# A state-space scan whose small matmuls move between the products of a projection

## The reference

```
proj = h @ w_in[layer]
u, q, k, v, f_logit, g_ssm, g_att = jnp.split(proj, IN_SPLITS, axis=-1)
...
xr = jnp.einsum('blgh,gph->blgp', ug, br)
xi = jnp.einsum('blgh,gph->blgp', ug, bi)
...
_, _, sr, si = lax.associative_scan(_complex_affine_combine, (lr, li, xr, xi), axis=1)
y = (jnp.einsum('blgp,ghp->blgh', sr, c_re.astype(f32))
     - jnp.einsum('blgp,ghp->blgh', si, c_im.astype(f32)))
y = y.reshape(bsz, seq, SSM_WIDTH) + d_skip.astype(f32) * u32
y = jax.nn.gelu(y).astype(u.dtype)
```

## Time and profile before

| | us |
|---|---|
| median of 3 runs | 3455.22 (3454.71 to 3459.01) |
| profiled execution, span | 3463.4 |
| entry and scan, up to the last product of turn 7 | about 208 of it |
| PE busy over the whole span | 3252.7 (94%) |
| PE idle at the start of the scan stage | 6.9 |
| PE waiting for POOL at turn 4 | 3.3 |

### The profile page before, as it was taken

One profiled execution on the slowest core, in us unless ns is written; L12 is line 12 of the kernel. 1 busy time (PEld: TensorE's weight loads), 2 busy tenths in 40 slices (PEclk: granted clock), 3 DMA queues, 4 the chain that ended last, 5 costly groups with the idle time before them and its releaser, 6 DMA issues. The chain is left out here.

```text
span 3463.4 us, 48142 instructions
## 1 busy us (share of the span) xinstructions
PE 3252.7 (94%) x16380; PEld 2680.7 (77%) x16380; DVE 1826.3 (53%) x3756; ACT 1303.2 (38%) x2179; POOL 1334.0 (39%) x830
## 2 busy tenths in 40 slices
PE   7999999898889999999999987899999988999999
PEld 6867787798888888888888854478888864478887
DVE  7404324887748777777777377432212336642211
ACT  4234433245543333333334334333322215633322
POOL 2323352288862222222221323434444316734443
PEclk9889999999999999999999998799999988999999
DMA  5321242244569999999997310023323420023332
GB/s 121 81 70 32 73 109 75 60 153 172 197 240 341 323 325 317 332 317 325 322 321 242 82 49 25 9 83 97 97 85 99 118 55 1 1 86 97 97 90 80
DMA packets 453881, 502.00 MB, mean 145 GB/s; under 512 B 77409, under 2 KB 398241, under 8 KB 435825
## 3 DMA queue, kind: packets, MB, share of 16 engines
q1 hardware_dynamic: 430448, 363.77, 34.3%
q0 software_dynamic: 18432, 134.23, 10.5%
q10 hardware_dynamic: 4864, 2.23, 0.3%
HBM read 458.06 MB, written 38.80 MB: 143 GB/s over the span
## 5 line engine op out<-in xcount | busy, mean ns | idle before, releaser
L125 POOL TENSOR_TENSOR w_low<-w_ring,w_high 128x1024 fp32r<-128x1024 f32 (+3 forms) x317 | 758.2, 2395 | 1136.4 <-ACT w_high L120 1108.8
L136 PE MATMUL ps<-h_low,w_high 128*128 128x512 f32 (+1 forms) x2432 | 918.5, 378 | 54.1 <-POOL w_low L125 28.3
L137 PE MATMUL ps<-h_high,w_high 128*128 128x512 f32 (+1 forms) x2432 | 900.6, 370 | 0.0
L138 PE MATMUL ps<-h_high,w_low 128*128 128x512 f32 (+1 forms) x2432 | 900.5, 370 | 0.0
L136 PEld LDWEIGHTS ps<-h_low,w_high 128*128 128x128 f32 x2432 | 464.0, 191 | 125.9 <-POOL w_low L125 31.8
L137 PEld LDWEIGHTS ps<-h_high,w_high 128*128 128x128 f32 x2432 | 463.9, 191 | 63.8 <-issue 6.3
L138 PEld LDWEIGHTS ps<-h_high,w_low 128*128 128x128 f32 x2432 | 462.9, 190 | 56.9
L120 ACT ACTIVATE w_high<-w_ring 128x1024 fp32r<-128x1024 f32 (+3 forms) x317 | 323.9, 1026 | 123.6 <-PE ps L138 120.0
L136 PE MATMUL ps<-v_low,top 128*128 128x512 f32 x768 | 299.7, 390 | 6.6 <-DVE v_low L125 6.6
L138 PE MATMUL ps<-v_high,top_at 128*128 128x512 f32 x768 | 300.8, 392 | 0.0
L137 PE MATMUL ps<-v_high,top 128*128 128x512 f32 x768 | 300.7, 392 | 0.0
(11 more groups left out here) (538 smaller groups left out, 5452.7 us busy)
## 6 DMA issues: line engine op xcount, KB each, us to landing
w_ring<-in_peer_uv_dram SPq DMA_DIRECT2D x128, 512.0 KB
u_raw<-in_peer_uT_dram SPq DMA_DIRECT2D x78, 512.0 KB, 6.0
w_ring<-in_peer_uT_dram SPq DMA_DIRECT2D x50, 512.0 KB, 3.8
gates<-peer_gates SPq DMA_DIRECT2D x31, 768.0 KB, 11.4
w_ring<-in_ffn_w_gate_dram SPq DMA_DIRECT2D x44, 512.0 KB, 3.7
w_ring<-in_ffn_w_up_dram SPq DMA_DIRECT2D x44, 512.0 KB, 3.7
w_ring<-in_w_in_dram SPq DMA_DIRECT2D x36, 512.0 KB, 3.8
w_ring<-in_ffn_w_down_dram SPq DMA_DIRECT2D x32, 448.0 KB, 3.8
```

Of the source, the lines that this page charges most:

```text
L125: return eng.tensor_tensor(rounded(low), whole, high, ALU.subtract)
L136: nc.tensor.matmul(out, rounded(w_high), rounded(x_low), start=start, stop=False, **more)
L137: nc.tensor.matmul(out, rounded(w_high), rounded(x_high), start=False, stop=False, **more)
L138: return nc.tensor.matmul(out, rounded(w_low), rounded(x_high), start=False, stop=stop, **more)
```

## The change

`product` gets an argument `beside`, a function that is called behind each of its first two matmuls and that the tile loop calls twice more behind the third. Through it the 64 matmuls of the kernel stand in the two tiles of turn 1, four to a k step, and the 96 matmuls of the outputs in both tiles of turn 5 and the first of turn 6. The last k step's third matmul signals the tile before the small ones behind it. ACT moves the kernel after turn 1 (`move_kernel`), issues the band after turn 2 and does the gelus after turn 6. On DVE the product of the skip weights goes first, into another buffer, and the fill and the addition go between the steps up and the steps down. The read of u moves from the end of the entry to the head of SP's stream in the scan (`load_u`), ahead of the weight loads. The wait for `y_saved` moves from the end of the scan to `load_y`. Since pieces of work now stand around most turns, the turns are written out, all but turns 3 and 4.

```
-def product(nc, out, w_high, w_low, x_high, x_low, start, stop, **more):
+def product(nc, out, w_high, w_low, x_high, x_low, start, stop, beside=None, **more):
     nc.tensor.matmul(out, rounded(w_high), rounded(x_low), start=start, stop=False, **more)
+    if beside is not None:
+        beside(0)
     nc.tensor.matmul(out, rounded(w_high), rounded(x_high), start=False, stop=False, **more)
+    if beside is not None:
+        beside(1)
     return nc.tensor.matmul(out, rounded(w_low), rounded(x_high), start=False, stop=stop, **more)
...
-                mm.then_inc(mm_done, 1)
+                                 beside=(lambda at, i=i, b=b, k=k: beside[i, b](pe, 4 * k + at)) if given else None)
+                    if k == w.kt[b] - 1:
+                        mm.then_inc(mm_done, 1)
+                    if given:
+                        beside[i, b](pe, 4 * k + 2)
+                        beside[i, b](pe, 4 * k + 3)
...
-            sp.wait_ge(u_saved, 16 * SSM_T)
-            by_group = u_dram.rearrange("t (g h) (r s) -> r h (t g) s", h=SSM_H, r=PH)
-            for r in range(PH):
-                at = (PH - 1 - r) * SSM_H
-                sp.dma_start(tb.u[at:at + SSM_H, :, :], by_group[r]).then_inc(tb.u_in, 16)
...
+        def kernel_of(tile):
+            def beside(pe, at):
+                n = 32 * tile + at
+                p, x, two = n // 4, n // 2 % 2, n % 2
+                half = HALF[two]
+                mm = nc.tensor.matmul(c.ps[:, 6 + two, p * SSM_H:(p + 1) * SSM_H], tb.reach[half, x, p, :], tb.c[x][half, p, :], start=x == 0, stop=x == 1)
+                if p == PAIRS - 1 and x == 1:
+                    mm.then_inc(kernel_done, 1)
+            return beside
+
+        def load_u(sp):
+            sp.wait_ge(tb.u_saved, 16 * SSM_T)
+            by_group = tb.u_dram.rearrange("t (g h) (r s) -> r h (t g) s", h=SSM_H, r=PH)
+            for r in range(PH):
+                at = (PH - 1 - r) * SSM_H
+                sp.dma_start(tb.u[at:at + SSM_H, :, :], by_group[r]).then_inc(tb.u_in, 16)
...
+        def outputs_of(tile):
+            def beside(pe, at):
+                n = 32 * tile + at
+                p, part = n // 6, n % 6
+                if n == 0:
+                    pe.wait_ge(banded, 16 * PH)
+                    pe.wait_ge(moved, 4)
+                if n == 2:
+                    pe.wait_ge(carried, 2)
+                    pe.wait_ge(swept, total[0])
...
-        project_copy(c, w_qk, qkT, ahead, before={"dve": sweeps}, after={"sp": lambda sp: sp.wait_ge(y_saved, 16 * 4)},
-                     between={1: {"pe": fill, "act": move}, 4: {"act": band}, 6: {"pe": outputs, "act": gelus}})
+        project_copy(c, w_qk, qkT, ahead, before={"sp": load_u, "dve": sweeps},
+                     between={1: {"pe": fill, "act": move}, 2: {"act": move_kernel}, 3: {"act": band}, 5: {}, 6: {}, 7: {"act": gelus}},
+                     beside={(1, 0): kernel_of(0), (1, 1): kernel_of(1), (5, 0): outputs_of(0), (5, 1): outputs_of(1), (6, 0): outputs_of(2)})
...
         def load_y(sp):
+            sp.wait_ge(y_saved, 16 * 4)
```

More of the change, by code:

```diff
@@ L462, with project @@
 Programs = namedtuple("Programs", "sync gpsimd tensor scalar vector slots_free")
-def project(c, w, evacuate, rhs=None, ahead=None, whole=None, before={}, after={}, norm=None, between={}, unrolled=(), alternate=False):
+def project(c, w, evacuate, rhs=None, ahead=None, whole=None, before={}, after={}, norm=None, between={}, unrolled=(), alternate=False, beside=None):
     with c.stage() as ctx:
-        one = projection(c, ctx, w, evacuate, rhs, ahead, whole, before, after, norm, between, unrolled, alternate)
+        one = projection(c, ctx, w, evacuate, rhs, ahead, whole, before, after, norm, between, unrolled, alternate, beside=beside)
         with c.nc.Block() as block:
@@ L769, in tile_of, with project_copy @@
     return buf[:, i * per_turn + b, :]
-def project_copy(c, w, dest, ahead=None, before={}, after={}, norm=None, between={}):
+def project_copy(c, w, dest, ahead=None, before={}, after={}, norm=None, between={}, beside=None):
     nc = c.nc
@@ L780, in act @@
             split(b)
-    project(c, w, {"act": act}, ahead=ahead, before=before, after=after, norm=norm, between=between)
+    project(c, w, {"act": act}, ahead=ahead, before=before, after=after, norm=norm, between=between, beside=beside)
 def project_scaled(c, w, dest, ahead=None, before={}):
@@ L1847, in ssm @@
         entry(c, A, tables, w_u, w_qk, qkT)
-        scan(c, tables, w_qk, ahead, qkT, ygT, y_dram)
+        scan(c, tables, w_qk, ahead, qkT, ygT, y_dram, y_saved)
 class EntryNorm:
@@ L2143, in entry, with scan @@
                 after={"pe": lambda pe: turn(pe, range(KD, GROUPS)), "act": rest_moved, "sp": store_u})
-def scan(c, tb, w_qk, ahead, qkT, ygT, y_dram):
+def scan(c, tb, w_qk, ahead, qkT, ygT, y_dram, y_saved):
     nc = c.nc
@@ L2173, in fill @@
                         mm.then_inc(filled, 1)
-            for p in range(PAIRS):
-                for x in range(2):
-                    for two, half in enumerate(HALF):
-                        mm = nc.tensor.matmul(c.ps[:, 6 + two, p * SSM_H:(p + 1) * SSM_H], tb.reach[half, x, p, :], tb.c[x][half, p, :], start=x == 0, stop=x == 1)
-                        if p == PAIRS - 1 and x == 1:
-                            mm.then_inc(kernel_done, 1)
+        def kernel_of(tile):
[13 more added lines that the diff above has]
+                sp.dma_start(tb.u[at:at + SSM_H, :, :], by_group[r]).then_inc(tb.u_in, 16)
         def move(act):
@@ L2270, in sweeps @@
                 all_step(level, False)
+            dve.wait_ge(kernel_out, 2)
+            v.memset(tb.toeplitz, 0.0).then_inc(cleared, 1)
+            dve.wait_ge(diagonal, 1)
+            v.tensor_tensor(tb.kernel[0:SSM_H, :, :], tb.kernel[0:SSM_H, :, :], mine, ALU.add).then_inc(diagonal, 1)
             for level in range(LEVELS - 2, -1, -1):
```

62 lines of the change are left out of this document (28 added, 34 removed).

## The result

| | before | after |
|---|---|---|
| median of four runs each | 3456.12 us | 3521.55 us (3519.21 to 3523.30) |
| ratio | | 1.0181 (95% interval 1.0166 to 1.0195) |
| profiled execution, span | 3463.4 us | 3517.4 us |
| ACT's first squares of q and k, in the next stage, from the span's start | 217.85 us | 283.58 us |

The account below looks back on a forecast made before the run. PE was taken as the bound, held up by blocks of small matmuls that lower its clock and by waits. Terms -2.6 + 31.6 - 0.6 - 3.7 = +24.7 us gave 3480 us, own range 3470 to 3490, with rivals 3454 to 3508.

Parts of the forecast that it names:

- entry, turn 0 starts: End of the entry: with the reads of u behind the barrier, the next stage starts earlier, -2.6 us, bounds 0 to -2.6.
- turn 1 with its slow tail: Turn 1 with kernel matmuls in slots: the clock falls to 0.50 after 4.6 us; 21.6 becomes 53.2 us, +31.6.
- POOL's wait and its slow stretch: PE's 3.28 us wait for POOL and the slow clock behind it mostly go: -3.7 us, bounds -4.9 to 0.
- outputs with their slow tail: Three output tiles with matmuls in slots: 51.8 becomes 51.2 us, -0.6, if the clock stays up.
- I take the clock as staying up, just more likely than not: Outputs: full clock assumed because small matmuls are longer and a third have the products' shape; at 0.50, +27 us.
- third rival: The clock falls in the outputs too: up to +27 us more, 3508 us, or 3494 if midway; chance 0.28.
- slot's price: Small matmuls between products: 0.46 us for one kernel matmul, 0.51 for two; at clock 0.50, 0.66 and 0.77.
- the loads: Turn 1's weight loads behind u's eight reads (4.8 us of SP): costed at nothing, covered by 22.8 us.
- second rival: Full clock throughout, in turn 1 too: +5.4 us, 3461 us, not told from no change; chance 0.13.
- DVE's slack: Outputs wait for DVE's sweeps: 26 us with the fill against 33 us of turns 2 to 4; slack 7, cost nothing.
- weight load 0.32 us after its product's start: Sign to look for: a 64-row matmul's weight load starts about 0.32 us after its product's start, not with it.
- first rival: Switches hide: loads of the other shape run behind products, 0.056 us an instruction; -27.6 us, 3428 us; chance 0.12.

Follow-up runs that it names:

- the run with the kernel in a block: The changed kernel with the kernel's 64 matmuls back in a block behind the span states, the outputs still beside the products: 3487.29 us, 1.0075 of before.
- u read second: The changed kernel with all four small matmuls behind the third product and SP's reads of u behind turn 1's weight loads: 3441.20 us, 0.9954 of before.
- the run with 128: The changed kernel with the same slots, but kernel and carry matmuls taking all 128 array rows, not 64 (time only): 3447.37 us, 0.9968 of before.

## Why the prediction was wrong, step by step

The sign was right, and so was the mechanism in turn 1: a slot's switch, and the clock that falls with it. The forecast had the clock wrong in the outputs and took a slot as too cheap: +25 forecast, +65 measured, outside the range. By stages, from the two traces (and the earlier trace rows):

| term | predicted | measured |
|---|---|---|
| entry, turn 0 starts (58.59, now 56.48) | -2.6 | -2.1 |
| fill, to the first kernel matmul or turn 1 | 0 | +3.8 |
| turn 1 with its slow tail (21.6, now 56.7 + 1.8) | +31.6 | +36.9 |
| POOL's wait and its slow stretch | -3.7 | -4.9 |
| outputs with their slow tail (51.8, now 80.0 + 2.6) | -0.6 | +30.7 |
| behind them, to the next stage | 0 | +1.3 |
| sum | +24.7 | +65.7 |

**The step that failed** is "I take the clock as staying up, just more likely than not" in the outputs. It fell 13.7 us in and stayed at 0.50 for 66 us. That is the prediction's third rival, chance 0.28, priced at up to +27 more; it measured 31.3 more than the forecast's term. The reason given was that the small matmuls are longer there and a third has the products' shape. It did not hold the clock: in the run with the kernel in a block it went after 5.6 us, as in turn 1 (5.7). For turn 1 I had taken the block's behaviour as nearest; the same reading for the outputs, whose block fell within 3.7 us, would have given 3508, the upper end of the range. What puts the measured time above that end are the two terms that follow, the slot's price (5.3 us in turn 1 and some 4 in the outputs) and the loads (3.8).

**The slot's price** was mis-sized. Slot by slot, product to product less a product alone (0.23 and 0.43):

| slot | predicted, full | measured | predicted, 0.50 | measured |
|---|---|---|---|---|
| one kernel matmul | 0.46 | 0.52 | 0.66 | 0.83 |
| two | 0.51 | 0.53 | 0.77 | 0.84 |
| one carry | 0.49 | 0.56 | 0.71 | 0.91 |
| one on u | 0.28 | 0.25 to 0.36 | 0.33 | 0.42 to 0.45 |

At the full clock the estimate from attention's 2-row matmuls was 0.02 to 0.07 short for the matmuls of 64 rows. At 0.50 it was 0.07 to 0.20 short. For a single kernel matmul the sum had 0.41 us from its load to the next product, taken from a block, and 0.53 were seen (110.98 to 111.51); the rest of the 0.17 lies before the load, where I had kept the 0.09 us. That in a block the neighbours hide part of a small matmul's load is my reading, which no run tests. Fourteen k steps of turn 1 at 3.79 us in place of 3.38 are 5.7 us, the whole miss of that term. With the outputs at 0.50 throughout, three k steps take 11.04 us and not 9.86.

How the loss divides, by an estimate from these distances: at the full clock throughout, the slots as measured would make turn 1 36.2 us (48 x 0.75, +14.6) and the outputs 54.1 (8 x 6.76, +2.3). So of the 67.6 us of both terms 17 are switches and 51 the lower clock; the second rival's 3461 would have been 3470 even so.

**The loads.** "I cost that at nothing" was wrong by 3.8 us: 2.5 of more waiting for `reachT`, and the rest the transposes at the low clock behind it. The cover of 22.8 us was counted for PE's want of the weights; but ACT wants them first, at 64.44, 18 us ahead of PE's turn 1 (82.57), and stands in front of the moves of `reachT`. I named what was queued behind the reads on SP, not what was queued behind the late weights on ACT. Nor is it so that nobody wants u until the fill is over: the span states, inside the fill, read it (1.6 us of PE's wait in u read second).

**POOL** went as said, at the end of its bounds: no PE wait for it, -4.9. **DVE's slack** held: the last step down ends at 168.8 and the outputs start at 173.7, 5 us for the 7 predicted. **Turn 0** is earlier by 2.1 for 2.6. The sign "weight load 0.32 us after its product's start" was seen at 0.43. The first rival, switches that hide behind the products, is refuted: a small load of 64 rows starts 0.43 us after its product's start, where the next product in a row would have started at 0.23. The Trainium skill ("TensorE: Matmul & The Clock Gate", Step-by-step) says that PE pulls weight loads ahead of matmuls in flight when the row groups don't conflict or the load targets the background weight buffer. The traces agree where the rows are equal, 0.08 us after the product's start in the run with 128; between products of 128 rows and matmuls of 64 no load is seen ahead, and no run shows which of the two conditions is missing. The Trainium skill ("TensorEngine Tiling (Array Packing)", Key Properties) also says that a change of the tiling mode drains TensorE. The traces agree with that: a single slot costs 0.52 us with the change and 0.22 without.

## What to carry to other kernels

Small matmuls put between large ones cost mostly by changes of shape, there and back: at the full clock 0.5 us for one or two of 64 rows here, 0.25 us for each further two, and 0.22 us for one that has the products' rows. So if they have to stand among products, let them stand in longer rows, but not too densely: rows of eight and twelve behind every second and third k step kept the clock at 1.00 here, rows of 32 and rows of eight behind every k step did not. Before trusting a mix look at the granted clock in the nearest block of such work: what a mix costs at the lower clock is the number to plan with. And when a transfer is moved ahead of another, ask which engine waits for the second one first and what it has queued behind. And a point in one trace tells less than its digits say: the same code ahead of turn 1 ended 4.9 us apart in two traces.

## What was not expected of the hardware

- One and two small matmuls on the two halves of the array's rows cost the same between products (0.75 and 0.76 us with the product).
- The same output tiles kept a clock of 1.00 for 13.7 us in one kernel and for 5.6 in another that differs only ahead of them; with eight 16-column matmuls behind each k step the clock fell, with six of 63 and 64 columns it didn't, nor with four of 16.
- Eight reads with small pieces (128 KB each) ahead of two weight loads made these 4.8 to 6.9 us late at their reader in six traces, though SP had issued the last read at 61.4 us in the changed kernel's; with the loads issued first they were there in time in all five.
- In the same six traces PE waited 1.3 to 3.5 us for `reachT`. In the four with 2.0 us and more its clock read 0.50 for some of the time behind the wait, in the two with 1.3 and 1.7 it stayed at 1.00.
